# A conditioned decoder step on one Trainium2 core: how much of w_ada is multiplied unsplit, and in which order the head loads its weights

## What is computed

```python
sc = jax.nn.silu(c)                                   # 9 conditioning rows of 1024
mod = sc @ P['w_ada'][l] + P['b_ada'][l]              # w_ada: 1024 x 6144
sh1, s1, g1, sh2, s2, g2 = jnp.split(mod[:, None, :], 6, axis=-1)
h = _rmsnorm(x, P['norm1_g'][l]) * (1 + s1) + sh1     # x: 512 and 8 rows of 1024
m, na, nb, nc = _mixer(h, ...)                        # z = h @ w_in (1024 x 6144), three causal branches, w_o
x = x + g1 * m
h = _rmsnorm(x, P['norm2_g'][l]) * (1 + s2) + sh2
x = x + g2 * _moe(h, ...)                             # 16 experts, 2 of one group of 4 for each row
y = _rmsnorm(x, P['final_g'])
```

## Time and profile before

| | |
|---|---|
| median of three runs | 870.14 us (869.19 to 872.73) |
| the profiled execution | 871.01 us |
| its span in the trace | 869.3 us |
| its mean granted TensorE clock | 0.988 of full |
| TensorE matmul busy | 837.7 us, 96% of the span |
| VectorE busy | 684.0 us, 79% |
| ScalarE busy | 465.3 us, 54% |
| start of the first product of `w_in` | 47.78 us |

### The profile page before, as it was taken

The page is one execution under the profiler, slowest core; times in us unless marked ns, Lnnn a source line. Parts: engine busy times, 40 slices in busy tenths (PEclk is TensorE's granted clock), DMA queues, the critical chain, the costliest instruction groups (busy, mean ns, idle before and its releaser), DMA issues.

```text
span 869.3 us, 14877 instructions
## 1 busy us (share of the span) xinstructions
PE 837.7 (96%) x5035; PEld 699.5 (80%) x5035; DVE 684.0 (79%) x937; ACT 465.3 (54%) x555; POOL 77.0 (9%) x71
## 2 busy tenths in 40 slices
PE   7899999999999999999999899999999999999994
PEld 2589999989999999899777457888888888887861
DVE  0681638878798679599438889999989999899887
ACT  4552442343322222642222456888888888888852
POOL 0002000000000000230000001000000001003750
PEclk9879999999999999999999999999999999999998
DMA  9858545445454322123571479988896899999962
GB/s 330 274 156 274 208 131 166 142 153 168 146 151 123 97 73 74 45 84 123 209 278 75 167 244 398 400 341 302 316 400 212 323 398 399 400 400 398 364 218 98
DMA packets 90997, 201.24 MB, mean 232 GB/s; under 512 B 8792, under 2 KB 13400, under 8 KB 90918
## 3 DMA queue, kind: packets, MB, share of 16 engines
q1 hardware_dynamic: 78813, 165.25, 53.9%
q0 software_dynamic: 5136, 18.42, 5.9%
q10 hardware_dynamic: 7003, 16.95, 5.2%
HBM read 182.97 MB, written 18.35 MB: 232 GB/s over the span
## 4 chain that ended last, share of the span: by engine, by line
PE 80%; DVE 10%; ACT 3%; DMA 3%; issue 2%; ACTq 1%; SPq 0%; POOL 0%; POOLq 0%; DVEq 0%
PE ps L804 32%; PE ps L655 12%; PE ps L657 12%; PE ps L656 12%; PE ps L884 3%; DVE w_lo L1605 2%; PE ps L999 2%; DMA region_b<-h_rows,slot_idx 1%; PE ps L683 1%; ACT w_hi L1146 1%; PE ps L725 1%; PE ps L684 1%; PE ps L836 1%; PE ps L1034 1%; DMA region_b<-expert_rows,slot_i 1%
## 5 line engine op out<-in xcount | busy, mean ns | idle before, releaser
L1605 DVE TENSOR_TENSOR w_lo<-raw,w_hi 128x1024 fp32r<-128x1024 f32 x202 | 241.6, 1225 | 99.8 <-ACT w_hi L1146 97.8
L1146 ACT ACTIVATE w_hi<-raw 128x1024 fp32r<-128x1024 f32 x202 | 207.8, 1056 | 198.0 <-PE ps L804 150.6
L655 PE MATMUL ps<-w_hi,hT_hi 128*128 128x512 f32 (+1 forms) x512 | 205.5, 401 | 3.4 <-DVE w_lo L1605 1.4
L657 PE MATMUL ps<-w_hi,hT_lo 128*128 128x512 f32 (+1 forms) x512 | 202.1, 395 | 0.0
L656 PE MATMUL ps<-w_lo,hT_hi 128*128 128x512 f32 (+1 forms) x512 | 201.5, 394 | 0.0
L804 PE MATMUL ps<-hT_hi,w_hi 128*128 128x260 f32 x768 | 156.6, 285 | 1.5 <-DVE w_lo L1605 0.9
L804 PE MATMUL ps<-hT_hi,w_lo 128*128 128x260 f32 x768 | 155.0, 283 | 0.0
L804 PE MATMUL ps<-hT_lo,w_hi 128*128 128x260 f32 x768 | 155.0, 283 | 0.0
L804 PEld LDWEIGHTS ps<-hT_hi,w_hi 128*128 128x128 f32 x768 | 119.0, 190 | 4.8 <-DVE w_lo L1605 3.9
L804 PEld LDWEIGHTS ps<-hT_lo,w_hi 128*128 128x128 f32 x768 | 119.5, 190 | 0.0
L804 PEld LDWEIGHTS ps<-hT_hi,w_lo 128*128 128x128 f32 x768 | 118.9, 189 | 0.0
(11 more groups left out here) (345 smaller groups left out, 836.7 us busy)
## 6 DMA issues: line engine op xcount, KB each, us to landing
raw<-in_exp_w_dram SPq DMA_DIRECT2D x96, 512.0 KB
region_a<-in_exp_w_dram SPq DMA_DIRECT2D x80, 512.0 KB
raw<-in_w_in_dram SPq DMA_DIRECT2D x48, 512.0 KB
raw<-in_w_ada_dram SPq DMA_DIRECT2D x30, 512.0 KB
expert_rows<-region_b ACTq DMA_DIRECT2D x17, 512.0 KB, 6.5
region_b<-in_exp_w_dram SPq DMA_DIRECT2D x16, 512.0 KB
region_b<-in_w_ada_dram SPq DMA_DIRECT2D x14, 512.0 KB, 8.7
expert_rows<-region_a POOLq DMA_DIRECT2D x8, 512.0 KB, 9.0
```

The source lines that it names most:

```text
L655: pe.matmul(out, pairs[0], moving[0], start=start, stop=False)
L657: return pe.matmul(out, pairs[1], moving[0], start=False, stop=stop)
L1146: act.activation(w_hi[:, split_slot(n), :], place, ACT.Copy).then_inc(hi_done, 1)
L1605: return dve.tensor_tensor(out, whole, first.bitcast(F32), ALU.subtract)
```

## The change

Only group 0 of `w_ada` stays native (`G_NAT` = 1). Groups 1, 2 and 3 are split, so the head has 4 native and 12 split quarters, where it had 8 and 8.

The order of the loads: native 0 and 1, split 0 and 1 (into the places outside the ring, `nat_place[0]` and `[1]`, now without a wait), x_sample, x_prompt, native 2 and 3, split 2 to 7 into the ring, split 8 to 11 as ring places come free, and then `w_in`.

ScalarE and VectorE split quarters 0 and 1 ahead of the squares of x. A new semaphore `x_rooted` lets ScalarE scale x tiles 2 and 3 while VectorE scales the sample tile and tiles 0 and 1. Copies of turned x are interleaved with the splits. The parameter rows are turned ahead of x and not behind it, the sample rows behind quarter 3, both into bank 7. The turns of groups 0, 1 and 2 come as soon as each is complete, and the shift (`shift_out`) is formed on its own ahead of the scale. `dec_in` and `xsT` move to region_a. In the gap behind the router only the loads' counts change.

The diff, cut to its core:

```diff
-G_NAT = 2
+G_NAT = 1
+ADA_BANK = (4, 7, 5)
@@ sync
-            for h in range(6):
-                native(h)
+            native(0)
+            native(1)
+            quarter(0)
+            quarter(1)
             sp.dma_start(x_in[0:ND, 4, :], ...)
             for i in range(NP // P):
                 sp.dma_start(x_in[:, i, :], ...)
-            for h in range(6, 4 * G_NAT):
-                native(h)
-            for n in range(N_MIX):
+            native(2)
+            native(3)
+            for n in range(N_APART, N_MIX):
...
-                if n < N_APART:
-
-                    sp.wait_ge(nat_used, n + 1)
-                elif n >= RAW + N_APART:
+                if n >= RAW + N_APART:
@@ tensor
             pe.wait_ge(turned_out, 1)
-            for h in range(6):
-                native_quarter(h)
+            native_quarter(0)
+            native_quarter(1)
+            turn_params()
+            pe.wait_ge(cT_split, 2)
+            ada_quarter(0, 4)
+            ada_quarter(1, 4)
             head_running(28)
-            for h in range(6, 4 * G_NAT):
-                native_quarter(h)
+            native_quarter(2)
+            native_quarter(3)
             pe.wait_ge(xn_ready, NTILE)
             for k in range(4):
                 turn_x(k, k)
-            pe.wait_ge(cT_split, 2)
-            ada_quarter(0, 4)
-            ada_quarter(1, 4)
+            ada_quarter(2, 4)
             for k in range(4, KD):
                 pe.wait_ge(xT_out, k - 3)
                 turn_x(k, k - 4)
-            ada_quarter(2, 4)
             ada_quarter(3, 4)
+            turn_sampled()
+            ada_quarter(4, 7)
             pe.wait_ge(xT_out, KD)
-            turn_params()
-            ada_quarter(4, 7)
+            turn_mod(0, 0, 0)
             ada_quarter(5, 7)
             pe.wait_ge(fold_ready, 1)
-            for g in range(3):
-                t = turn_mod(g, 0, 36 * g)
-            t.then_inc(modT_done, 1)
+            turn_mod(1, 0, 36).then_inc(modT_done, 1)
             ada_quarter(6, 7)
             ada_quarter(7, 7)
+            ada_quarter(8, 5)
+            turn_mod(2, 1, 0).then_inc(modT_done, 1)
+            for n in range(9, N_HEAD):
+                ada_quarter(n, 5)
@@ scalar
-            native_out(0)
+            hi(0)
+            hi(1)
             for n, i in enumerate((4, 0, 1, 2, 3)):
...
-            hi(0)
-            hi(1)
-            for k in range(4):
-                turned_x(k)
-            native_out(1)
+            for i in (2, 3):
+                act.wait_ge(x_rooted, 1)
+                act.activation(x_in[:, i, :], x_in[:, i, :], ACT.Copy, scale=sums[:, 3, i:i + 1]).then_inc(xn_ready, 1)
             hi(2)
+            native_out(0)
+            turned_x(0)
+            turned_x(1)
             hi(3)
...
@@ vector
+            lo(0)
+            params_out()
+            lo(1)
             mean_squares()
             norm_root()
-            for t in range(NTILE):
+            dve.sem_inc(x_rooted, 1)
+            for t in (4, 0, 1):
                 dve.tensor_scalar(x_in[0:rows(t), t, :], ...).then_inc(xn_ready, 1)
-            for n in range(5):
-                lo(n)
-            params_out()
-            mod_group(2)
+            lo(2)
+            lo(3)
+            sampled_out()
+            lo(4)
+            mod_group(1)
             lo(5)
             lo(6)
+            shift_out()
             lo(7)
+            lo(8)
+            mod_group(2)
+            lo(9)
             scale_out(0)
             sampled_input(0)
             prompt_sum(0)
+            lo(10)
             sampled_rest(0)
             prompt_rest(0)
-            lo(8)
+            lo(11)
+            lo(N_HEAD)
```

More of the change, by code:

```diff
@@ L280, in trunk_step @@
         ld_x = sem("ld_x")
+        x_rooted = sem("x_rooted")
         x_landed = [sem(f"x_landed{i}") for i in range(NTILE)]
-        nat_ready = [sem(f"nat_ready{h}") for h in range(4 * G_NAT)]
+        nat_ready = [sem(f"nat_ready{h}") for h in range(4 * G_GAP)]
         apart_ready = [sem(f"apart_ready{n}") for n in range(N_APART)]
@@ L1185, in input_prompt @@
                 act.activation(hT_hi[:, k, 0:NP], xnT[:, k, :], ACT.Identity, bias=shiftT[:, k, ND:ND + 1], scale=scaleT[:, k, ND:ND + 1]).then_inc(hT_hi_done, 1)
[L1187 to L1191 removed]
+            for i in (2, 3):
+                act.wait_ge(x_rooted, 1)
+                act.activation(x_in[:, i, :], x_in[:, i, :], ACT.Copy, scale=sums[:, 3, i:i + 1]).then_inc(xn_ready, 1)
             hi(2)
+            native_out(0)
+            turned_x(0)
+            turned_x(1)
             hi(3)
[L1194 to L1195 removed]
+            turned_x(2)
+            turned_x(3)
             hi(4)
+            turned_x(4)
+            turned_x(5)
             hi(5)
[L1198 to L1199 removed]
+            turned_x(6)
+            turned_x(7)
+            for n in range(6, N_HEAD):
+                hi(n)
             act.wait_ge(xT_out, KD)
@@ L1202, in _ @@
             input_prompt(0)
-            hi(8)
+            hi(N_HEAD)
             input_prompt(1)
@@ L1210, in _ @@
                 input_prompt(k)
-            hi(10)
-            hi(11)
-            for n in range(N_HEAD + 4, N_HEAD + 7):
+            for n in range(N_HEAD + 2, N_HEAD + 7):
                 hi(n)
@@ L1656, in norm_root, with shift_out @@
                 rsqrt(sums[:, 1, 0:NTILE], sums[:, 2, 0:NTILE], sums[:, 3, 0:NTILE], sums[:, 2, 0:NTILE], 1)
+            def shift_out():
+                dve.wait_ge(modT_done, 1)
+                for h in range(2):
+                    dve.tensor_tensor(shiftT[:, 4 * h:4 * h + 4, :], ps[:, 0, 36 * h:36 * h + 36].rearrange("p (k s) -> p k s", s=9),
+                                      pT[:, :, R_BIAS + h:R_BIAS + h + 1].broadcast_to([P, KW, ND + 1]), ALU.add)
             def scale_out(half):
-                dve.wait_ge(modT_done, half + 1)
+                dve.wait_ge(modT_done, half + 2)
                 ks = slice(4 * half, 4 * half + 4)
@@ L1663, in row @@
                     return pT[:, :, r + half:r + half + 1].broadcast_to([P, KW, ND + 1])
-                if half == 0:
-                    for h in range(2):
-                        dve.tensor_tensor(shiftT[:, 4 * h:4 * h + 4, :], ps[:, 0, 36 * h:36 * h + 36].rearrange("p (k s) -> p k s", s=9),
-                                          pT[:, :, R_BIAS + h:R_BIAS + h + 1].broadcast_to([P, KW, ND + 1]), ALU.add)
-                turned_scale = ps[:, 0, 72:108] if half == 0 else ps[:, 6, 0:36]
+                turned_scale = ps[:, 6, 0:36] if half else ps[:, 1, 0:36]
                 link(dve.tensor_tensor(scaleT[:, ks, :], turned_scale.rearrange("p (k s) -> p k s", s=9), row(R_BIAS + 2), ALU.add))
@@ L1727, in _ @@
                 prompt_rest(k)
-            lo(10)
-            lo(11)
-            lo(N_HEAD + 4)
-            lo(N_HEAD + 5)
+            for n in range(N_HEAD + 2, N_HEAD + 6):
+                lo(n)
             dve.memset(ua[:, :, 0:CK - 1], 0.0)
```

32 lines of the change are left out of this document (15 added, 17 removed).

## The result

| | before | after |
|---|---|---|
| median | 869.85 us (867.51 to 872.73, 18 runs) | 872.59 us (868.80 to 875.86, 18 runs) |
| profiled execution | 871.01 | 874.57 |
| its span | 869.3 | 872.8 |
| mean granted clock | 0.988 | 0.985 |
| first product of `w_in` starts | 47.78 | 50.59 |

A forecast was written before the change was run, and what follows sets the result against it. TensorE bounds the kernel behind the head, so only the head's change counts: 871.0, less 2.0 for an earlier first product, plus 0.3 for a late half-rate spell, gives 869.3 us (early spell 869.1); range 866.3 to 872.8.

The forecast's parts named there:

- part 4: Head, walk from scaled x at 23.2 to the first product at 45.8, 2.0 us earlier.
- Parts 1 and 2: Head: x loaded two places forward, landing at 17.9, and its scaling shared, done at 23.2, not 27.1; gain 3.9 us.
- The walk's 30.1: Head: time when TensorE is done with the turns, quarter 3 and the sample rows' small transposes.
- the 2.0 of the forecast: Head: the first product of w_in starts 2.0 us earlier, taken off 871.0.
- Part 5: Loads of quarters 8 to 11 wait for ring places; up to 1 us late, covered, cost nothing.
- The bound of 14.0: Loads of quarters 8 to 11: 14.0 us from issue to landing with a full queue, 4.2 with an empty one.
- Part 6: TensorE's clock in the head: one or two half-rate spells; late one gives 869.3, early one 869.1.
- Half rate through the head: Rival: clock falls by 32 us and stays low into the first products; product at 50.5, time 873.7; chance 0.17.
- The clock holds: Rival: no clock fall in the head before the products run; 867.4 us; chance 0.20.
- x does not land sooner: Rival: shared DMA queue keeps x landing at 20.6, 2.7 us lost, product at 48.5; 872.0 us; chance 0.06.
- It gains more: Rival: head's two waits and two splits all hidden, 3.9 and 2.0 us both count; 865.1 us; chance 0.05.
- four signs that the prediction names for being wrong: x at 20 or later; ScalarE awaiting quarters 8 to 11; half clock from 32 to products; product-to-end distance changed over 2 us.

The follow-up runs named there:

- experiment 1: After with the parameter rows turned behind native quarter 3 on TensorE and copied behind the scaling on VectorE; 869.96 us, ratio to before 1.0006.
- experiment 5: Before with the parameter rows turned behind native quarter 1 and copied ahead of the splits; 873.33 us, ratio to before 1.0038.
- experiment 2: After without the 28 dummy transposes, the wait for the parameter rows left in place; 869.04 us, ratio to before 0.9997.
- experiment 11: Experiment 4's kernel with VectorE scaling all five tiles of x, the two ScalarE scalings taken out; 869.14 us, ratio to before 0.9991.
- experiment 8: Before with five dummy transposes ahead of quarter 4 and nine ahead of quarter 5; 867.95 us, ratio to before 0.9979.
- experiment 4: Experiment 1 with ten dummy transposes ahead of quarter 4; 866.95 us, ratio to before 0.9971.
- experiment 7: Experiment 4 with sample rows turned behind quarter 4 and copied behind split 5, shift behind split 7; 866.24 us, ratio to before 0.9951.
- experiment 6: Before with x loaded behind four native quarters, not six; 873.65 us, ratio to before 1.0043.
- experiment 10: Experiment 6 without its 28 dummy transposes; 870.68 us, ratio to before 1.0014.

## Why the prediction was wrong

**The step that failed** is the clause on `turn_params`: the front part says that the parameter rows are now turned ahead of x, and part 4 of the prediction starts its walk from 23.2 with "TensorE: turns, quarter 3" and prices nothing that TensorE has queued ahead of them. I took it for granted that what stands ahead of x is done by then. A step moved forward needs its inputs sooner, and I did not ask when these land. The trace of before could not show it directly: there the turn comes at 34.8 and waits for nothing. Its loads' start was to be seen, on a queue beside a full one (384 GB/s even at 26 us), and the lateness could have been bounded by the 9.3 us median of the quarters' loads: issued by 5.66, in by about 15. Instead of that bound the sum had zero. What the runs showed in its place: a wait of 3.47 us, from 11.85 to 15.32, which moves the first product from 46.11 to 50.59. It is worth 1.8 to 2.6 us of the time (experiment 1, ratio and medians) and 3.3 when put into before (experiment 5), and it took the dummies to make it so (experiment 2). The second step that failed is the yardstick, under part 4.

**Parts 1 and 2** were right to 0.4 us at the landing and to 0.1 at the three times behind it. The price of ScalarE's scaling, 1.06 each from the nearest row, is 2.19 for two. Sharing is worth 0.6 us at the first sum (experiment 11).

**Part 4**, without the failed step, was right too: experiment 1 starts the product at 46.11 (forecast 45.8), and its VectorE idles 2.11 us at the sample rows (1 to 2) and 1.08 at the shift (0.8). (The walk's 30.1 is 0.4 more than its terms, 28.1 + 0.92 + 0.66, give; the copy came at 29.81.) But the gain that I read from it, 47.78 - 45.8, compares a walk at the upper clock with a row that holds a half-rate stretch. At the same clock before starts at 45.23 (experiment 8) and the mended change at 45.35 (experiment 4). In these two x is scaled by 26.55 and 23.0, 3.5 us apart; the first sum ends at 42.38 and 41.19, 1.2 apart; at the product nothing is left. So what parts 1 and 2 gain is not half but wholly taken back: 2.4 us ahead of the sum, where the change's VectorE waits 2.10 for the sample rows, and 1.3 behind it, where the two more splits stand. (The front part has "five are added" ahead of the sum; its lists have eight splits there in both orders.) The medians are 867.95 and 866.95, 1.0 apart (0.7 by the ratios, whose intervals overlap), so a gain of the new order, mended, is not shown, and the 2.0 of the forecast were the clock's.

**Part 5** held: in after no wait of ScalarE for the loads of quarters 8 to 11 stands in its timeline up to the product, and in experiment 1, where all comes sooner, 0.54 us for quarter 11 (forecast: up to 1, covered). The bound of 14.0 is that of x; the quarters' own is 15.7.

**Part 6**, the clock: it fell as forecast in the thin stretches (34 to 38 and 48 to 52 in after), and earlier, at 14 to 20, in a wait that I had not seen. The size of a spell over the first products, 2.0 us, is near the 1.8 of experiment 8. What I did not see is that executions of one kernel differ by several us, with their clock (experiment 1: 0.983 to 0.995) and with the wait for the gathered rows: experiment 1's profile promised 866.9 and its median is 870.0.

**The rivals.** "Half rate through the head" named 50.5 for the product and 873.7 for the time, near the 50.59 and 874.57 of the profile, but not by its mechanism: between 21 and 34 us the clock was at its upper level in after, and the lateness was there by 27, at the turns of x. "The clock holds" is what experiment 4 made happen, at 866.95 where the rival said 867.4. "x does not land sooner" is refuted by the landing at 18.3. "It gains more" would have needed both waits and splits hidden; experiment 7 hides the waits and is at 866.24, not 865.1.

None of the four signs that the prediction names for being wrong came true: x is in by 18.3, no load of quarters 8 to 11 is waited for, the clock is back up between 38 and 48, and the product is 821.5 us ahead of the end before and 822.2 after. The signs watched the terms that the sum has, not the one that it lacks.

The range took the result in, since it reached to the slower rivals, whose mechanisms did not happen; that is luck. Its centre was 3 us too low.

## What to carry to other kernels

When a step moves forward, ask first when its inputs land, small ones on another queue included, and then what is queued behind it on its engine: a wait that is covered by itself turns expensive through filler work that stands behind it. Compare a walk at full clock only with rows at full clock, or the clock's loss is counted as the change's gain. Where short pieces alternate with waits of TensorE, filler can pay (1.3 us of it went with 3.0 here), but not behind a wait for a load that everything else is queued behind.

## What was not expected of the hardware

- Eight loads of 90 KB in all, on a queue of their own, were complete only at 14.3 (experiment 5), 15.3 and 15.4 us (after, experiment 2), about 9 to 10 us behind the last issue, while the DMA engines moved some 350 to 400 GB/s from 6 us on, nearly all of it for SyncE's queue. Which of them was last, and whether issue, turn-taking or landing takes the time, stays open.
- With ten transposes, 1.31 us, the granted clock stood at 1.00 in all stretches from 28 to 54 us in experiment 4, while its other stretches were as thin as those of experiment 1 (40 to 42: 0.89 us busy of 2, against 1.02), whose clock fell to 0.59 in 44 to 46. So one filled place goes with another course of the clock 15 us later; there is one profile of each, so that the filler did it is not shown; the medians, 866.95 and 869.96, go the same way.
- A spell at the lower level in the middle of the program stands in some profiles and not in others, with the same work there: between 480 and 500 us in after and experiments 2, 5, 6 and 10, between 510 and 520 in experiment 7, and near 520 in experiment 10 too. In after it moved the first gather by about 0.4 us.
- The wait for the second gather, zero in five profiles and up to 2.19 us (experiment 10) in the others, is as large as the effects measured here. What sets it was not looked into.
